# The MLP of a two-layer backbone's last layer, from exact fp32 matmuls to three rounded ones

## The reference

```python
def sq_relu_mlp(h, w1, w2):
    return jnp.square(jax.nn.relu(h @ w1)) @ w2
...
        x_l = x_l + g2_l * sq_relu_mlp(rms_norm(x_l, norm2_w[l]) * (1.0 + sc2_l) + sh2_l, mlp_w1[l], mlp_w2[l])
        if not last:
            x_c = x_c + g2_c * sq_relu_mlp(rms_norm(x_c, norm2_w[l]) * (1.0 + sc2_c) + sh2_c, mlp_w1[l], mlp_w2[l])
    return rms_norm(x_l, final_norm_w)
```

## Time and profile before

| what | value |
|---|---|
| runs of the kernel | 2950.54, 2955.51, 2956.82 us (median 2955.51) |
| profiled execution, first to last instruction | 2950.0 us (the page gives no other time of it) |
| TensorE busy | 2763.4 us, 94% |
| VectorE, ScalarE, GpSimd busy | 977.6, 659.3, 449.8 us |
| mean granted TensorE clock | 0.945 of full speed |
| layer 0's MLP on TensorE | from 1322.5 to about 1709 us |
| layer 1's MLP on TensorE | from 2712.6 to about 2938 us |

### The profile page before, as it was taken

How to read it: one execution, slowest core, us unless ns; L and a number is a source line. 1 busy time by engine, 2 the same in 40 slices (tenths; PEclk the granted TensorE clock), 3 DMA queues, 4 the chain that set the end, 5 groups by cost and what they waited for, 6 DMA issues and landing times. The chain is left out here.

```text
span 2950.0 us, 51713 instructions
## 1 busy us (share of the span) xinstructions
PE 2763.4 (94%) x22928; PEld 1959.7 (66%) x22928; DVE 977.6 (33%) x1594; ACT 659.3 (22%) x923; POOL 449.8 (15%) x567
## 2 busy tenths in 40 slices
PE   8999999999999899999999999999888998799998
PEld 2553847658449656646888757386685657688887
DVE  1323443544116422225444332345444215211000
ACT  3213122331120311122222241323323120301100
POOL 0002221312006400000000000313223107100100
PEclk9999999999996799999999999999998996899999
DMA  7312220201110012232222251201000030143441
GB/s 300 139 50 77 78 80 3 80 5 57 49 70 33 33 64 97 73 126 87 86 101 99 86 194 72 95 25 52 19 14 30 2 121 33 61 157 115 160 154 72
DMA packets 18222, 239.42 MB, mean 81 GB/s; under 512 B 2001, under 2 KB 3153, under 8 KB 3409
## 3 DMA queue, kind: packets, MB, share of 16 engines
q1 hardware_dynamic: 16128, 218.11, 19.7%
q10 hardware_dynamic: 1872, 18.02, 1.5%
HBM read 230.88 MB, written 5.24 MB: 80 GB/s over the span
## 5 line engine op out<-in xcount | busy, mean ns | idle before, releaser
L379 PE MATMUL psum<-normed,weight_ring 128*128 128x256 f32 (+1 forms) x2320 | 771.6, 492 | 32.5 <-DVE work L892 11.5
L379 PEld LDWEIGHTS psum<-normed,weight_ring 128*128 128x128 f32 x2320 | 449.3, 195 | 342.8 <-issue 274.5
L392 PE MATMUL psum<-work 64*64 64x64 f32 (+1 forms) x9088 | 307.7, 222 | 13.9 <-ACT work L1614 10.5
L392 PEld LDWEIGHTS psum<-work 64*64 64x64 f32 x9088 | 294.9, 135 | 25.4 <-issue 14.5
L435 PE MATMUL psum<-weight_ring,derived 128*2 128x512 f32 x384 | 169.5, 602 | 12.4 <-ACT derived L1460 9.6
L898 DVE SCALAR_TENSOR_TENSOR work<-psum,derived,work 128x256 f32<-128x256 f32 x96 | 46.4, 484 | 394.7 <-PE psum L859 218.7
L736 PE MATMUL psum<-work 128*128 128x64 f32 x672 | 139.6, 399 | 13.9 <-DVE work L1277 10.8
L736 PEld LDWEIGHTS psum<-work 128*128 128x128 f32 x672 | 135.3, 310 | 18.0 <-DVE work L1277 12.3
L1204 DVE TENSOR_TENSOR work<-work,psum 128x512 f32<-128x512 f32 x144 | 99.0, 688 | 142.0 <-PE psum L392 141.9
L1778 POOL TENSOR_TENSOR work<-work,constants 128x512 f32<-128x512 f32 x80 | 108.2, 1352 | 205.8 <-DVE work L1187 140.6
L794 PE MATMUL psum<-work,weight_ring 128*128 128x512 f32 (+1 forms) x384 | 131.6, 485 | 0.0
(11 more groups left out here) (229 smaller groups left out, 3929.8 us busy)
## 6 DMA issues: line engine op xcount, KB each, us to landing
weight_ring<-in_weights SPq DMA_DIRECT2D x78, 2048.0 KB, 7.9
weight_ring<-in_weights SPq DMA_DIRECT2D x16, 2304.0 KB, 8.6
weight_ring<-in_weights SPq DMA_DIRECT2D x10, 1536.0 KB, 6.6
x_scratch<-work ACTq DMA_DIRECT2D x2, 2048.0 KB, 11.5
work<-x_scratch ACTq DMA_DIRECT2D x2, 2048.0 KB, 9.0
work<-in_ret_constants ACTq DMA_DIRECT2D x2, 1152.0 KB, 14.5
work<-in_small_weights ACTq DMA_DIRECT2D x2, 1152.0 KB, 5.2
work<-in_x ACTq DMA_DIRECT2D x1, 2048.0 KB, 26.1
```

The source lines that it names most:

```text
L379: last = mm(ps[:, 0:t1 - t0], tiled(s, j, k), hT[:, k, t0:t1], start=(k == 0), stop=(k == KT - 1))
L392: last = mm(ps[q, w * m:w * m + w], lhs(q, m), rhs(q, m), start=True, stop=True)
```

## The change

Layer 1's MLP takes the form of layer 0's, on 256 columns in place of 512. The slots of its weights become the 16 of `mlp_slots`, in the order m1, m1, m2, m2. Each of its 512 weight tiles is multiplied by three rounded matmuls. ScalarE and VectorE split each of the 16 slots. VectorE takes over relu and square from ScalarE and GpSimd, and each hidden tile and each of the 8 normed tiles is split too. The sums of `m2` become 32 sums of 8 tiles in place of 8 sums of 32. Number and size of the transfers stay as they are. `w` is 256 in layer 1.

```diff
@@ schedule_slots
-        if l < L - 1:
-            for n, key in enumerate(mlp_slots(l)):
-                out += [(key, 4 * KT * P)]
-                if n == 1:
-                    ada("mlp", l)
-        else:
-            out += [(("m1", l, a), 4 * KT * P) for a in range(8)]
-            out += [(("m2", l, f), 32 * P) for f in range(8)]
+        for n, key in enumerate(mlp_slots(l)):
+            out += [(key, 4 * KT * P)]
+            if n == 1:
+                ada("mlp", l)
@@ TensorE
-                for n, key in enumerate(mlp_slots(l) if l < L - 1 else ()):
+                for n, key in enumerate(mlp_slots(l)):
...
-                                hi = normed_hi[:, k, :]
-                                mm(ps, w_hi, hi, start=(k == 0), stop=False)
-                                mm(ps, w_hi, hT_r[:, k, :], start=False, stop=False)
-                                last = mm(ps, s[:, P * t:P * t + P], hi, start=False, stop=(k == KT - 1))
+                                hi = normed_hi[:, k, t0:t1]
+                                mm(ps[:, 0:w], w_hi, hi, start=(k == 0), stop=False)
+                                mm(ps[:, 0:w], w_hi, hT_r[:, k, t0:t1], start=False, stop=False)
+                                last = mm(ps[:, 0:w], s[:, P * t:P * t + P], hi, start=False, stop=(k == KT - 1))
...
-                for f in range(32 if l == L - 1 else 0):
-                    if f % 4 == 0:
-                        s = slot("m1", l, f // 4)
-                    project(s, f % 4, ("m1", l, f), t0, t1, 2 if f == 0 else None)
-                for f in range(KT if l == L - 1 else 0):
-                    s = slot("m2", l, f)
-                    ps = big.fill("m2", l, f)
-                    eng.wait_ge(*big.freed())
-                    for k in range(32):
-                        if f == 0:
-                            eng.wait_ge(pool_mlp.sem, pool_mlp.at("hidden", l, k))
-                        last = mm(ps[:, 0:t1 - t0], s[:, P * k:P * k + P], work[:, hid(k) + t0:hid(k) + t1],
-                                  start=(k == 0), stop=(k == 31))
-                    last.then_inc(big_filled.sem, big_filled.step(("m2", l, f)))
-                    norm_behind(l, 3, f)
@@ VectorE: tail, output projection, MLP
-                    if which == 2 and l < L - 1 and k >= 2:
+                    if which == 2 and k >= 2:
                         normed_low(l, k - 2)
...
-                    if f == 5 and l < L - 1:
+                    if f == 5:
                         weights_low(l, 0)
...
-                for n, (kind, _, a) in enumerate(mlp_slots(l) if l < L - 1 else ()):
+                for n, (kind, _, a) in enumerate(mlp_slots(l)):
                     if n < 15:
                         weights_low(l, n + 1)
...
-                            t = wk(HID_T + 512 * (f % 2))
-                            ps = big.get("m1", l, f)
+                            t = wk(HID_T + 512 * (f % 2), w)
+                            ps = big.get("m1", l, f)[:, 0:w]
@@ ScalarE
-                for n_, (kind, _, a) in enumerate(mlp_slots(l) if l < L - 1 else ()):
+                for n_, (kind, _, a) in enumerate(mlp_slots(l)):
                     if n_ < 15:
                         weights_high(l, n_ + 1)
                     for f in range(4 * a, 4 * a + 4) if kind == "m1" else ():
                         eng.wait_ge(vec_mlp.sem, vec_mlp.at("squared", l, f))
-                        act(hidden_hi[:, f % 8, :], wk(HID_T + 512 * (f % 2)), ACT.Copy).then_inc(
+                        act(hidden_hi[:, f % 8, t0:t1], wk(HID_T + 512 * (f % 2), w), ACT.Copy).then_inc(
                             act_mlp.sem, act_mlp.step(("hidden high", l, f)))
...
-                for f in range(32 if l == L - 1 else 0):
-                    eng.wait_ge(big_filled.sem, big_filled.at("m1", l, f))
-                    act(work[:, hid(f) + t0:hid(f) + t1], big.get("m1", l, f)[:, 0:n], ACT.Relu).then_inc(act_mlp.sem, act_mlp.step(("drained", "m1", l, f)))
-                    eng.wait_ge(act_mlp.sem, act_mlp.n)
@@ GpSimd
-                for k in range(KT if l < L - 1 else 0):
+                for k in range(KT):
 
                     eng.wait_ge(act_norm.sem, act_norm.at("h tile", l, 2, k))
-                    nc.gpsimd.tensor_copy(normed_hi[:, k, :], hT[:, k, :]).then_inc(
+                    nc.gpsimd.tensor_copy(normed_hi[:, k, t0:t1], hT[:, k, t0:t1]).then_inc(
                         pool_mlp.sem, pool_mlp.step(("normed high", l, k)))
-                    eng.wait_ge(pool_mlp.sem, pool_mlp.n)
-                for f in range(32 if l == L - 1 else 0):
-                    eng.wait_ge(act_mlp.sem, act_mlp.at("drained", "m1", l, f))
-                    h_ = work[:, hid(f) + t0:hid(f) + t1]
-                    tt(h_, h_, h_, ALU.mult).then_inc(pool_mlp.sem, pool_mlp.step(("hidden", l, f)))
                     eng.wait_ge(pool_mlp.sem, pool_mlp.n)
```

More of the change, by code:

```diff
@@ L838, in _ @@
                                     eng.wait_ge(vec_mlp.sem, vec_mlp.at("hidden", l, 8 * q + k))
[L839 to L842, removed]
+                                hi = hidden_hi[:, k, t0:t1]
+                                mm(ps[:, 0:w], w_hi, hi, start=(k == 0), stop=False)
+                                mm(ps[:, 0:w], w_hi, hidden_lo[:, k, t0:t1], start=False, stop=False)
+                                last = mm(ps[:, 0:w], s[:, P * t:P * t + P], hi, start=False, stop=(k == KT - 1))
                             last.then_inc(big_filled.sem, big_filled.step(("m2", l, q, f)))
                             if q == 3:
[L845 removed]
+                                norm_behind(*((l + 1, 1) if l < L - 1 else (l, 3)), f)
                     if n == 1:
                         modulation("mlp", l)
[L848 to L862 removed]
         @block.vector
@@ L921, in tail @@
                     eng.wait_ge(vec_norm.sem, vec_norm.n)
-                    if which == 2 and l < L - 1 and k >= 2:
+                    if which == 2 and k >= 2:
                         normed_low(l, k - 2)
-                if which == 2 and l < L - 1:
+                if which == 2:
                     normed_low(l, KT - 2)
@@ L930, in normed_low @@
                 eng.wait_ge(pool_mlp.sem, pool_mlp.at("normed high", l, k))
-                hi = normed_hi[:, k, :].bitcast(F32)
-                tt(hT_r[:, k, :], hT[:, k, :], hi, ALU.subtract).then_inc(vec_mlp.sem, vec_mlp.step(("normed split", l, k)))
+                u0, u1 = rspan(l)
+                hi = normed_hi[:, k, u0:u1].bitcast(F32)
+                tt(hT_r[:, k, u0:u1], hT[:, k, u0:u1], hi, ALU.subtract).then_inc(vec_mlp.sem, vec_mlp.step(("normed split", l, k)))
                 eng.wait_ge(vec_mlp.sem, vec_mlp.n)
@@ L1361, in _ @@
                             eng.wait_ge(act_mlp.sem, act_mlp.at("hidden high", l, f))
-                            hi = hidden_hi[:, f % 8, :].bitcast(F32)
-                            tt(hidden_lo[:, f % 8, :], t, hi, ALU.subtract).then_inc(vec_mlp.sem, vec_mlp.step(("hidden", l, f)))
+                            hi = hidden_hi[:, f % 8, t0:t1].bitcast(F32)
+                            tt(hidden_lo[:, f % 8, t0:t1], t, hi, ALU.subtract).then_inc(vec_mlp.sem, vec_mlp.step(("hidden", l, f)))
                             eng.wait_ge(vec_mlp.sem, vec_mlp.n)
@@ L1372, in _ @@
                         modulation("mlp", l)
-                for f in range(KT if l == L - 1 else 0):
-                    eng.wait_ge(big_filled.sem, big_filled.at("m2", l, f))
-                    add_gated(vec_mlp, big.get("m2", l, f), 40 + f, X + 512 * f, live(l), t0, ("drained", "m2", l, f))
             tail(L - 1, 3)
@@ L1413, in norm @@
                 for k in range(KT):
-                    if which == 2 and l < L - 1 and k == 5:
+                    if which == 2 and k == 5:
                         weights_high(l, 0)
@@ L1857, in last_use @@
             "m2q": lambda: ("m2", l, i[0] // 2, 4 * (i[0] % 2) + 3),
-            "m1": lambda: ("m1", l, 4 * i[0] + 3), "m2": lambda: ("m2", l, *i)}[kind]()
-def hid(f):
-    return 512 * f if f < 12 else 14336 + 512 * (f - 12)
+            "m1": lambda: ("m1", l, 4 * i[0] + 3)}[kind]()
 def wsm_up(work, wcol):
@@ L1958, in lay_out @@
             m = tiles(inp["mlp_w2"][l][D * q:D * q + D, BW * g:BW * g + BW])
-        else:
-            m = tiles(inp["mlp_w2"][l][:, P * a[0]:P * a[0] + P])
         w[i, :, :n] = m.reshape(P, n)
```

## The result

The changed kernel takes 2969.69 us (median of 4 runs, 2968.62 to 2971.75), the kernel before on the same chips 2953.03. The ratio is 1.0062, with a 95% interval of 1.0048 to 1.0077: slower by 0.6%. The prediction said 2970.5, range 2955 to 2990.

A forecast was written before the change was run, and what follows sets the result against it. TensorE bounds the kernel before; after, it waits for weight splitting ahead of drains. 2950.0 + 0.5 (matmul gain given back in waits) + 14.8 (clock) = 2965.3, plus 5.5 from span to median, given as 2970.5 us; range 2955 to 2990.

The forecast's parts named there:

- The working of the change: Layer 1's MLP: TensorE pauses before third sums in 14 slots, 3.4 us behind m1, 2.0 behind m2, waiting for splitting.
- Two terms put at nothing: Splitting the first slot during the output projection, and transfers issued one slot ahead, both costed at nothing.
- The pitch of the rounded matmul: Distance of 256-column rounded matmuls on TensorE: 0.1155 us, half the 0.2317 of 512 columns; a tile 0.3465 against 0.4315.
- bounds of 0.112 and 0.139: Matmul distance in us: lower from trains with short moving tiles, upper from a read rate shared by weights and moving tile.
- The two slot lengths: Slots 2 to 15: 14.4 us behind m1, 13.0 behind m2, against 13.81 before; together 0.3 us more.
- The start: First slot of layer 1's MLP: TensorE starts the second slot at 2731.5, 2.9 us later than before.
- The last slot: No splitting ahead of its drains: 11.1 us in place of 13.81, 2.7 less.
- The clock: Seven of eight 3.4 us pauses followed by 4.6 us at half clock: 14.8 us more, bounds 0 and 30.
- The clock holding: Rival, chance 0.18: full clock behind the pauses, +0.5 us with -2.9 to +5 by matmul distance, 2953 to 2961.
- The slow matmul: Rival, chance 0.10: rounded matmul does not halve at 256 columns; 2976 to 2984 at 0.139 us, 3090 at 0.2317.
- A TensorE-bound and faster kernel: Rival, chance 0.07: each slot's first drain comes within two sums' 5.5 us, so no pauses or clock price: 2917.
- the last addition: Profiled span forecast of 2965.3 plus 5.5 us from span to median of the runs, given as 2970.5.

The follow-up runs named there:

- half-splitting run: Changed kernel with each splitting operation of layer 1's MLP on 1024 columns in place of 2048, split tiles used twice, result differs: 2918.74 us, 0.9885 of the kernel before.
- order run: Changed kernel with layer 1's drains and weight splitting interleaved on VectorE, ScalarE's second high half moved in m1 slots, same two banks: 2924.50 us, 0.9911 of the kernel before.
- filled run: Changed kernel plus 16 unread rounded matmuls ahead of the third sum in eight slots behind m1 slots: 2954.19 us, 1.0014 of the kernel before.
- second execution: Changed kernel itself measured once more, nothing altered: 2966.58 us, 1.0055 of the kernel before, last stretch 257.8 us.
- deferred order: Reordered drains and splitting with two banks, plus VectorE splitting or draining before each low part instead of waiting for ScalarE's copy: 2912.71 us, 0.9874 of the kernel before.
- four-bank kernel: Changed kernel with layer 1's MLP sums in four other PSUM banks in place of two: 2937.37 us, 0.9948 of the kernel before.

## Why the prediction was right

**The working of the change.** Right. The pauses came in the places, in the number and behind the lines forecast: 15 ahead of third sums, eight long and six short in the 14 middle slots. The half-splitting run shows that the splitting ahead of the first drain is the cause, and the order run that its place in the order of VectorE and ScalarE is, not its size. Two terms put at nothing were right as well: splitting the first slot during the output projection held TensorE for nothing, and no wait of TensorE is put down to a transfer.

**The pitch of the rounded matmul.** Taken as 0.1155 us, measured 0.118 (17 in 2735.86 - 2733.86 = 2.00 us). The term was too small by 2%. The bounds of 0.112 and 0.139 were both valid, the upper far off. The prediction sets a figure of the Trainium skill beside it, page "TensorE: Matmul & The Clock Gate", section "Back-to-back issue gap", as one for a train; that section gives the formula for the gap of a single matmul in isolation, and it is the page's section "Wait — 56ns, not 53.3ns?" that gives it for matmuls back to back. Both measured distances lie above it, 232 ns where it gives 216 and 118 ns where it gives 109; no term of the sum hangs on it.

**The two slot lengths.** 14.4 and 13.0 us were forecast. At full clock (the filled run) they are 14.7 and 13.2, and a round of two and two lasts 55.84 us, not 54.9. The sum said that 14 slots change by +0.3 us (from unrounded lengths; the printed ones give 193.2 and not 193.6); with 0.94 more for each of 3.5 rounds it is +3.6. Half of that is the pitch (192 x 0.0023 = 0.44 a round). Most of the other half is a term that the sum does not have: the first matmul behind a pause holds the next up for 0.22 us and not 0.118 (2724.57 to 2724.79 in the changed kernel), four times a round.

**The start.** Forecast +2.9 us at the start of the second slot. Counted from the table load it lies at 2728.64 - 2707.71 = 20.9 before and 2730.34 - 2705.90 = 24.4 after: +3.5. TensorE ran the first slot at half clock until 2722 us, which the sum does not price. It cost nothing here, since TensorE then still waited 1.06 us for the drain.

**The last slot.** Forecast -2.7; 96 x 0.118 = 11.3 in place of 13.81 gives -2.5.

**The clock.** Forecast +14.8 us, from seven of eight pauses with 4.6 us at half clock. Seven of eight it was, and six of eight in the second execution. Each fall lasted 3.4 or 6.8 us, part of it inside the pause, so slow streaming behind one was 3.0 to 5.9 us, a mean of 4.3. Measured by it, the clock cost 13.5 us, and 11.0 in the second execution; the filled run prices it at 3.65 us a round, 12.8 over 3.5 rounds, and at 2.75 or 9.6. The size was right within the scatter of two executions. That it would be seven no row of the kernel before could say; the number was a choice between none and fourteen.

Together: 3.5 + 3.6 + 13.5 - 2.5 = 18.1, where the last stretch grew by 17.9 us. In the second execution 3.5 + 3.6 + 11.0 - 2.5 = 15.6, where it grew by 15.5. The forecast sum was 15.3. Part of the closeness of the median (2969.7 against 2970.5) is luck: the terms without the clock were 4.1 us low, the clock was 1.3 to 3.8 us high, and what lies ahead of the stretch came out 1.8 us shorter. There is a slip in the last addition besides: 2965.3 and 5.5 are 2970.8. The 5.5 us from the profiled span to the median were 3.6 in the changed kernel (2969.69 - 2966.1).

**The rivals.** The clock holding is what the filled run looks like, and its last stretch of 246.7 us lies 4.4 above before, where the rival said up to 5. The slow matmul is out. A TensorE-bound and faster kernel was priced at 2917: the kernel with half of the splitting came to 2918.7, and the price was right, but the change as made does not reach the condition for it. The deferred order does, and better (2912.7): its last stretch is 3.6 us shorter than with half of the splitting, most of it in the eight slots behind `m1` slots (11.3 us each in place of 11.6 to 11.7), the rest in the first slot.

The Trainium skill's "FP8 and Floating Point Precision", section "TensorE Precision Notes", counts four passes for a true fp32 product against the three of this form. The gain is there once the pauses are gone: 242.3 - 206.2 = 36 us. The prediction's estimate from it was 55 us, with 0.107 us for a pass; with the measured 0.4315 us for a tile in fp32 and 3 x 0.118 for the rounded form it is 512 x 0.0775 = 40 us. The Trainium skill's "TensorE: Matmul & The Clock Gate", section "A second HAM failure mode: psum-queue depth-cycling", tells of throughput lost to the clock when TensorE idles between groups of matmuls. The long pauses here agree with it: they cost 11.0 to 13.5 us of clock on top of their own length. The six pauses of 1.60 to 1.71 us do not: none was followed by half clock.

## What to carry to other kernels

When a matmul gets shorter, look at what its length was hiding: here two sums of 11.1 us covered a splitting that does not depend on the columns, and at 256 columns two sums last 5.7 us. In a program written out in order, put the step that frees a bank ahead of the step that prepares the next tile, and put a wait for another engine behind work of one's own; both together cost no computing instruction more and turned +0.6% into -1.3%. In this kernel a pause of TensorE of 3.1 us cost about half as much again in clock (two of them a round, and 2.75 to 3.65 us a round more). And price the part that changed by itself when the rest of the kernel varies more than the effect.

## What the runs showed of the hardware that I had not expected

- The rounded matmul's distance at 256 columns (0.118 us) is nearly half of that at 512 (0.2317). At half clock it is 0.213 us, which is 256 columns at 1.2 GHz. At full clock 256 columns would be 0.107 us and 512 would be 0.213, so the surplus is 11 and 18 ns: neither the same nor quite in proportion.
- Whether the clock falls behind a pause of 3.1 us is not settled by its length: of 16 such pauses in two executions of the changed kernel 13 were followed by half clock and three were not. None of that kernel's pauses between slots of up to 1.7 us was, nor was one of 2.0 us in the first slot of its second execution. But two pauses of 1.3 us with 0.6 us of work between them (the four-bank kernel, 2745.8 to 2749.1 us) were followed by 3.4 us at 0.50.
- Adding 128 useless matmuls made the kernel 12 us faster (1.0014 against 1.0055 of the kernel before).
- Behind the pause of the norm TensorE runs at half clock for 7.6 to 9.7 us of the first slot in every form with rounded matmuls, the best one too (7.6); in the kernel before it was 4.6 us. No run prices this in the best form.
